# Block sums of the MLP's down weights accumulated in the slots of the blocks, and their difference formed by VectorE

## What is computed

```
def sq_relu_mlp(h, w_up, w_down):
    return jnp.square(jax.nn.relu(h @ w_up)) @ w_down
...
    for l in range(DEPTH):
        ...
        x = x + sq_relu_mlp(rmsnorm(x, g_mlp[l]), w_up[l], w_down[l])
```

## Time and profile before

| | |
|---|---|
| median of 3 runs | 2283.35 us (2280.56 to 2287.49) |
| the profiled execution | 2282.37 us |
| its span | 2280.2 us, 28188 instructions |
| PE busy | 2224.9 us (98%) |
| DVE, ACT, POOL busy | 1251.0 (55%), 952.6 (42%), 354.6 us (16%) |
| granted TensorE clock, mean | 0.993 |
| software queue of POOL's DMAs | 39.09 MB, 8.9% of 16 engines |
| hardware queue of SP's DMAs | 201.67 MB, 34.0% |

### The profile page before, as it was taken

How to read it: one execution, slowest core, us unless ns; L and a number is a source line. 1 busy time by engine, 2 the same in 40 slices (tenths; PEclk the granted TensorE clock), 3 DMA queues, 4 the chain that set the end, 5 groups by cost and what they waited for, 6 DMA issues and landing times.

```text
span 2280.2 us, 28188 instructions
## 1 busy us (share of the span) xinstructions
PE 2224.9 (98%) x11733; PEld 1853.4 (81%) x11733; DVE 1251.0 (55%) x1891; ACT 952.6 (42%) x1372; POOL 354.6 (16%) x319
## 2 busy tenths in 40 slices
PE   7799999999999999999999999999999999999998
PEld 6468889888876678898988878888888888888887
DVE  3874655674236646565656675554333446465553
ACT  5664433433225635344344574542322343233343
POOL 0561100002200011000021303332101211000020
PEclk9899999999999999999999999999999999999999
DMA  4204768643460026966636345334345333333331
GB/s 159 83 1 149 176 173 221 162 120 105 134 190 25 1 88 151 238 170 146 187 61 93 47 37 64 49 47 74 65 102 93 98 87 96 108 93 103 92 111 56
DMA packets 233083, 242.55 MB, mean 106 GB/s; under 512 B 8392, under 2 KB 192148, under 8 KB 232829
## 3 DMA queue, kind: packets, MB, share of 16 engines
q1 hardware_dynamic: 214621, 201.67, 34.0%
q0 software_dynamic: 18304, 39.09, 8.9%
q10 hardware_dynamic: 32, 0.01, 0.0%
HBM read 238.62 MB, written 4.74 MB: 107 GB/s over the span
## 4 chain that ended last, share of the span: by engine, by line
PE 80%; DVE 8%; DMA 6%; ACT 4%; issue 1%; POOL 1%; SPq 0%; DVEq 0%; ACTq 0%; POOLq 0%
PE bank L630 21%; PE bank L632 21%; PE bank L631 20%; PE bank L2654 5%; PE bank L2840 2%; DVE weight_lo L616 2%; DMA weight_raw<-in_w_down 2%; DMA bias<-in_w_down 2%; DMA mlp_room<-in_w_down 2%; ACT weight_hi L607 2%; PE bank L953 2%; PE bank L1981 1%; PE bank L804 1%; PE bank L814 1%; DVE dsa_latents L1307 1%
## 5 line engine op out<-in xcount | busy, mean ns | idle before, releaser
L630 PE MATMUL bank<-h_hi,weight_hi 128*128 128x512 f32 (+1 forms) x1568 | 615.8, 393 | 4.7 <-DVE h_lo L736 3.6
L632 PE MATMUL bank<-h_hi,weight_lo 128*128 128x512 f32 (+1 forms) x1568 | 612.2, 390 | 0.0
L631 PE MATMUL bank<-h_lo,weight_hi 128*128 128x512 f32 (+1 forms) x1568 | 611.8, 390 | 0.0
L616 DVE TENSOR_TENSOR weight_lo<-weight_raw,weight_hi 128x2048 fp32r<-128x2048 f32 (+5 forms) x163 | 341.6, 2097 | 289.1 <-ACT weight_hi L607 288.9
L607 ACT ACTIVATE weight_hi<-weight_raw 128x2048 fp32r<-128x2048 f32 (+5 forms) x166 | 287.7, 1735 | 229.3 <-PE bank L632 190.0
L630 PEld LDWEIGHTS bank<-h_hi,weight_hi 128*128 128x128 f32 (+1 forms) x1568 | 294.5, 188 | 68.5 <-issue 7.3
L632 PEld LDWEIGHTS bank<-h_hi,weight_lo 128*128 128x128 f32 (+1 forms) x1568 | 294.4, 188 | 63.2
L631 PEld LDWEIGHTS bank<-h_lo,weight_hi 128*128 128x128 f32 (+1 forms) x1568 | 294.7, 188 | 61.3
L630 PE MATMUL bank<-hidden_hi,weight_hi 128*128 128x256 f32 (+1 forms) x800 | 241.0, 301 | 11.6 <-DVE weight_lo L616 9.3
L632 PE MATMUL bank<-hidden_hi,weight_lo 128*128 128x256 f32 (+1 forms) x800 | 239.2, 299 | 0.0
L631 PE MATMUL bank<-hidden_lo,weight_hi 128*128 128x256 f32 (+1 forms) x800 | 238.7, 298 | 0.0
(11 more groups left out here) (446 smaller groups left out, 3455.3 us busy)
## 6 DMA issues: line engine op xcount, KB each, us to landing
weight_raw<-in_w_down SPq DMA_DIRECT2D x32, 1024.0 KB, 5.7
weight_raw<-in_w_up SPq DMA_DIRECT2D x44, 512.0 KB, 4.8
weight_raw<-in_w_up SPq DMA_DIRECT2D x20, 1024.0 KB, 7.4
weight_raw<-in_w_in SPq DMA_DIRECT2D x20, 1024.0 KB, 9.6
weight_raw<-in_w_down POOLq DMA_DIRECT2D x14, 1024.0 KB, 10.3
weight_raw<-in_w_in SPq DMA_DIRECT2D x24, 512.0 KB, 8.7
bias<-in_w_down SPq DMA_DIRECT2D x10, 1024.0 KB, 8.5
mlp_room<-in_w_down SPq DMA_DIRECT2D x10, 1024.0 KB, 7.4
```

What stands on the lines that cost most here:

```text
L616: dve.e.tensor_tensor(split_flat(v, 1), raw_flat(v), f32(split_flat(v, 0)), ALU.subtract).then_inc(*split.mark(("unit", v)))
L630: pe.e.matmul(o, w[0], x[0], start=start, stop=False, skip_group_check=onto)
L631: pe.e.matmul(o, w[0], x[1], start=False, stop=False, skip_group_check=onto)
L632: return pe.e.matmul(o, w[1], x[0], start=False, stop=stop, skip_group_check=onto)
```

## The change

Three things are changed, and a fourth follows from the slots.

1. The order of the blocks becomes n2, n6, m3, n4, m1, m5, m7. SP loads only the first four. m1 is the difference of the raw units m3 and n4, formed by DVE into n2's slot (`vector_difference`), behind the remainder of chunk 7; ACT's negation is gone. m5 and m7 are m3's and n4's raw units with W(0,1) added onto each in place. POOL issues these two DMAs when the difference is made and m3 (for m5) or n4 (for m7) is split. So a step has four loads by SP and four accumulating DMAs.
2. For the last chunk, `remainder(s, c - 1)` stands ahead of `relu(s, c)`.
3. The raw slots have fixed roles a, b, c, d within a step; a and b are exchanged after each step. The four down units of step 3 use all four slots.
4. The reload of `bias` waits for the splits of the first two down units of step 3, in place of splits of its up units.

```
-FAST_BLOCKS = ("n2", "n6", "n4", "m1", "m3", "m5", "m7")
+FAST_BLOCKS = ("n2", "n6", "m3", "n4", "m1", "m5", "m7")
...
                 if block and roles is None:
                     at = (at + at % 2) % (2 * N_RAW)
-                    roles = [N_RAW, N_RAW + 1, at // 2, 1 - at // 2]
-                if block or (name[0] == "up" and name[2]):
-                    slot = roles[0]
-                    roles = roles[1:] + roles[:1]
+                    roles = N_RAW, N_RAW + 1, at // 2, 1 - at // 2
+                last_downs = name[0] == "down" and not block
+                if block or last_downs or (name[0] == "up" and name[2]):
+                    a, b, c, d = roles
+                    slot = ({"n2": a, "n6": b, "m3": c, "n4": d, "m1": a, "m5": c, "m7": d}[block] if block else
+                            roles[name[3]])
                     halves = [2 * slot, 2 * slot + 1]
                     before[u] = [last[2 * slot]] if last[2 * slot] is not None else []
-                    at = 2 * slot if slot < N_RAW else at
+                    if block == "m7":
+                        roles, at = (b, a, c, d), 2 * c
...
-            if block == "m1":
+            if block and block not in first_block:
                 return
-            earlier = [v for v in range(u % (2 * N_RAW), u, 2 * N_RAW) if fast_block(v) != "m1"]
+            earlier = [v for v in range(u % (2 * N_RAW), u, 2 * N_RAW) if not fast_block(v) or fast_block(v) in first_block]
...
-        def scalar_negated(act, u):
-
-            act.wait_ge(*landed(u - 1))
+        def vector_difference(dve, u):
+
+            dve.wait_ge(*landed(u - 2))
+            dve.wait_ge(*landed(u - 1))
             for before in raw_before[u]:
-                act.wait_ge(*split.when("unit", before))
-            act.e.activation(raw_flat(u), raw_flat(u - 1), ACT.Copy, scale=-1.0).then_inc(*negated.mark(("unit", u)))
+                dve.wait_ge(*split.when("unit", before))
+            dve.e.tensor_tensor(raw_flat(u), raw_flat(u - 2), raw_flat(u - 1), ALU.subtract).then_inc(*difference.mark(("unit", u)))
...
-            pool.wait_ge(*(negated.when("unit", u) if block == "m1" else landed(u)))
+            if block in first_block:
+                pool.wait_ge(*landed(u))
+            else:
+                pool.wait_ge(*difference.when("unit", unit_at[plan[u][0][:3] + ("m1",)]))
+                pool.wait_ge(*split.when("unit", u - 3))
...
-                    if c == NC - 2 and s < FAST_STEPS:
-                        scalar_negated(act, unit_at["down", layer, s, "m1"])
...
+                    if c == NC - 1:
+                        remainder(s, c - 1)
                     relu(s, c)
-                    if c:
+                    if 0 < c < NC - 1:
                         remainder(s, c - 1)
...
                 remainder(s, NC - 1)
                 if s < FAST_STEPS:
+                    vector_difference(dve, unit_at["down", layer, s, "m1"])
                     for before, name in zip(FAST_BLOCKS[1:], FAST_BLOCKS[2:]):
...
-            for n in (0, 3):
-                pool.wait_ge(*split.when("unit", unit_at["up", 0, FAST_STEPS, n]))
+            for n in range(2):
+                pool.wait_ge(*split.when("unit", unit_at["down", 0, FAST_STEPS, n]))
```

More of the change, by code:

```diff
@@ L459, in build_program @@
         tile_full, rounded, split = signal("tile_full"), signal("weight_rounded"), signal("weight_split")
-        negated, added_in = signal("weight_negated"), {block: signal(f"added_in_{block}") for block in ("n2", "n6", "m1", "m5", "m7")}
+        difference, added_in = signal("weight_difference"), {block: signal(f"added_in_{block}") for block in ("n2", "n6", "m5", "m7")}
         (setup, dsa, att0, mlp0, kv, nsa, mlp1, mix, fox, dn, rec, merge, ffn, ple) = (
@@ L541, in columns @@
             return [split_flat(u, half).rearrange("p (k n) -> p k n", k=kc)[:, k, c0:c1] for half in range(2)]
-        first_block = {"n2": (1, 0), "n6": (0, 0), "n4": (1, 1), "m3": (0, 0), "m5": (0, 0), "m7": (0, 1)}
-        added_block = {"n2": (1, 1), "n6": (1, 0), "m1": (0, 0), "m5": (0, 1), "m7": (1, 1)}
+        first_block = {"n2": (1, 0), "n6": (0, 0), "m3": (0, 0), "n4": (1, 1)}
+        added_block = {"n2": (1, 1), "n6": (1, 0), "m5": (0, 1), "m7": (0, 1)}
         def down_block(u, i, j):
@@ L582, in unit_ready @@
             block = fast_block(u)
+            if block == "m1":
+                return difference.when("unit", u)
             return added_in[block].when("unit", u) if block in added_block else landed(u)
-        def scalar_negated(act, u):
-            act.wait_ge(*landed(u - 1))
+        def vector_difference(dve, u):
+            dve.wait_ge(*landed(u - 2))
+            dve.wait_ge(*landed(u - 1))
             for before in raw_before[u]:
-                act.wait_ge(*split.when("unit", before))
-            act.e.activation(raw_flat(u), raw_flat(u - 1), ACT.Copy, scale=-1.0).then_inc(*negated.mark(("unit", u)))
+                dve.wait_ge(*split.when("unit", before))
+            dve.e.tensor_tensor(raw_flat(u), raw_flat(u - 2), raw_flat(u - 1), ALU.subtract).then_inc(*difference.mark(("unit", u)))
         def pool_added(pool, u):
             block = fast_block(u)
-            pool.wait_ge(*(negated.when("unit", u) if block == "m1" else landed(u)))
+            if block in first_block:
[3 more added lines that the diff above has]
+                pool.wait_ge(*split.when("unit", u - 3))
             pool.e.dma_start(raw_view(u), down_block(u, *added_block[block]), accum_op=ALU.add
```

## The result

The changed kernel takes 2291.31 us (median of 7 runs, 2289.53 to 2292.01), the kernel before in the same comparison 2282.25 us (7 runs, 2278.87 to 2287.49). The ratio is 1.0038, with a 95% interval of 1.0027 to 1.0049: slower by some 8.7 us. The range of the prediction held the time. The forecast had been +4.8 us, within 0.3% (6.9 us) of no change; the measured ratio lies just above that 0.3%, and its interval reaches across it.

What follows compares the result with a forecast made beforehand. PE, busy 98%, was taken as the bound, losing time to m7's late start, set by m5's issue. Later m7 starts (+2.0 us) and two more clock falls (+2.8) gave +4.8: 2288 us, range 2277.5 to 2294.

Steps and rivals of the forecast that it cites:

- The bound: Down phases: m5's DMA issue sets m7's start, at issue + about 18.2 + 4.38 us in the kernel before.
- The issue at 14.07 and 14.83: m5's DMA, released by DVE's difference, is issued 14.07 us after n2's first matmul, 14.83 in a layer's first step.
- The wait ahead of n4: PE newly waits 0.2 to 0.4 us for n4's split, queued behind the difference; n4 starts at about 17.35.
- The stall in n2: PE's wait for chunk 6's remainder, 0.6 us a phase, goes in four phases and stays in two.
- The pair of 18.0 us: m5's and m7's accumulating DMAs take 18.0 us from m5's issue to m7's round; bounds 17.0 and 18.5.
- The clock: Ahead of m7, PE idles 1.9 us, so its clock falls in four of six phases, two more than before: +2.8 us.
- The early remainder earns nothing: The 0.6 us won in n2 in four phases only makes PE come earlier to its wait for m7.
- The port: Rival: DVE holds up POOL's descriptors, m5's issue comes 3.1 us later per phase; +26 us, 2309; chance 0.03.
- the clock falls in all six: Rival: four new clock falls behind m7's wait, with a pair of 18.5 us; +10.6 us, 2294; chance 0.30.
- A pair shorter than 17.0 us: Rival: without SP's loads ahead, m5's and m7's DMAs take 17.0 us, no clock falls; -6.8 us, 2276.6; chance 0.10.

Runs made afterwards that it cites:

- e1: The changed kernel with DVE's difference moved ahead of the split of m3: 2270.33 us, 0.9952 of the kernel before.
- e4: The changed kernel with the difference formed twice, one behind the other: 2303.33 us, 1.0095 of the kernel before.
- e8: The kernel before, with SP's load of the next first up unit held back until m7's sum has landed: 2269.22 us, 0.9942 of the kernel before.
- e5: The changed kernel with SP's load of the next step's first up unit held until m7's accumulating DMA has landed: 2266.48 us, 0.9927 of the kernel before.
- e7: The changed kernel executed once more without an edit, for a second trace of the clock: 2289.99 us.
- e3: The kernel before with only the remainder of chunk 6 put ahead of the relu of chunk 7: 2282.21 us, 1.0004 of the kernel before.
- e2: The changed kernel with the remainder of chunk 6 put back behind the relu: 2292.42 us, 1.0052 of the kernel before.

## Why the prediction was right in part, point by point

**The bound: right.** The issue of m5 sets m7's start; moved forward (e1) or back (e4) it takes m7 with it.

**The issue at 14.07 and 14.83: right.** Measured are 14.05 to 14.12 in four phases, and 14.81 and 14.91 in the two first steps. Every term of that chain held to within 0.1 us, the hand-over to POOL too (0.37 for 0.35).

**The wait ahead of n4: right, on the low side.** PE starts it at 17.30 (forecast 17.35), after 0.17 us of idle, in the four phases that are not a layer's first; in the two others it does not wait there.

**The stall in n2: right.** It is gone in four phases and left in two.

**The pair of 18.0 us: the step that failed.** The sum had taken 18.0, with 18.5 as the upper bound, because SP's loads of m5 and m7 would no longer run ahead of the pair. The six pairs, from m5's issue to m7's landing, are 18.7, 18.6, 18.3, 18.4, 18.2 and 18.6 us, on average 18.5, where the same measure on the kernel before gives 18.4: nothing was won. At 0.46 us a phase that is 2.8 of the 3.1 us by which the starts of m7 came out later than forecast (+5.1 for +2.0). The reason given for it fell with e8: the same pair is as short as 14.1 us with those loads still there. Fewer bytes beside the pair did not help either: in the second phase SP's queue moved 2.33 MB between m5's issue and m7's landing before and 1.70 MB after, and the pair took 18.2 and 18.6 us. The working had seen that the up unit stays, and for it had kept the estimate near the pairs of the kernel before. But it had one up unit in view, where three are issued while the pair runs (the earlier trace rows show two in one line), and it did not ask what they cost: about 4 us by e5 and e8.

**The clock: the count right, the reason not.** Four falls of six were forecast for +2.8 us; there were four, for +3.1. But they had been counted from an idle just above 1.87 us, as by a limit in time; the idles are 2.2 to 2.7 us, and e7 shows that the same kernel has three falls in one execution and four in another. The number agreed partly by luck.

**The early remainder earns nothing: right for the kernel before, not for the changed one.** On the kernel before it changes nothing (e3). In the changed kernel the working had counted its 0.6 us in m5's issue (PE ends n2 sooner), and yet the text called it a gain of nothing; e2 shows that without it m7 is 1.9 us later over the six phases.

**The port: as argued.** POOL's issue took 1.27 us at 360.99, with DVE's additions under way and the split at 361.74 right behind. The warning of the Trainium skill ("SBUF — State Buffer", section "SBUF: two separate sides") does not show in this row, which agrees with the exception for tensor_tensor, as before.

**The rivals.** The pair of 18.5 us came true from "the clock falls in all six", the falls did not; that case gave 2294, the forecast 2288, and the runs lie between, at 2291.3. With the measured pair and four falls the sum of the prediction is 2.0 + 6 x 0.46 + 2.8 = 7.6 us, against 8.0 in the span. A pair shorter than 17.0 us exists, 13.6 to 15.6 us, but the change doesn't bring it: it takes the hold on SP.

## What to carry to other kernels

When an operation is put on an engine that follows a written order, look for the gap in that order which its inputs already allow. Here DVE idled 2.1 us a few lines earlier, and with the same subtraction behind that gap the change costs 8.7 us, ahead of it it gains some 11. And before fewer bytes are taken for a shorter transfer, ask what runs beside the one transfer that is waited for: six accumulating DMAs and twelve loads less did not make that pair shorter, while holding SP's next up units back until it has landed, by some 12 us for the first of them, gained 25 us on the changed kernel and 13 on the one before.

## What the runs showed of the hardware

Two accumulating DMAs of 1 MB, issued 2.6 to 5.5 us apart, land 18.0 to 19.6 us after the first issue where SP's loads of the next up units run beside them (seven traces), and 13.6 to 15.6 us where these are held back (four traces). In the second phase m5 landed 9.3 us after its issue in the changed kernel and 9.7 with the units held; m7 then took another 9.2 us in the one and 5.0 in the other. The up loads beside it thus cost the second DMA some 4 us. The DMA engines are busy for only six tenths of the whole stretch from n2 to m7, but in the second phase of the changed kernel for 0.94 of the time in which the pair is under way, and not at all ahead of it: the mean over the stretch hides that they are full just where m7 waits for them.

The granted clock of TensorE fell from 1.00 to a mean of 0.76 to 0.79 over the block behind the idle (partly 1.2 in place of 2.4 GHz) after idles of 2.20, 2.29, 2.48, 2.56, 2.71, 3.18 and 3.60 us in the two traces of the changed kernel. It did not after 2.29, 2.42, 2.53, 2.56 and 2.59 us, and the two traces differ in the phases in which it fell. In the other traces it fell after idles down to 1.87 us (kernel before) and did not after 3.22 us (e4). A fall cost 1.4 to 1.5 us in these two traces; in e2 one block took 8.47 us and so lost 2.7. Whoever counts falls in such a sum should give them a spread and not a limit.
